# Latent attention and retention as steps between the first projection's weight tiles, and high parts of the tokens written straight from the PSUM banks

## The reference

```python
h = rms_norm(x, attn_norm_w)
r_q, r_k, r_v, r_g, c_q, c_kv, k_pe = split(h @ w_in)   # widths 4 x 512, 256, 128, 32
# retention, 8 heads of 64: decayed scores times values, norm of each head, gate
q, k = rope(r_q), rope(r_k) / 8
o = ((q @ k.T) * decay_mask) @ r_v                      # written here for both chunks at once
y_ret = silu(r_g) * group_norm(o) * ret_gn_w
# latent attention, 8 heads of 64 + 32
q = rms_norm(c_q) @ w_uq;  kv = rms_norm(c_kv) @ w_ukv
s = (q_nope @ k_nope.T + rope(q_pe) @ rope(k_pe).T) * 96 ** -0.5   # causal
y_mla = softmax(s) @ v
x = x + concat(y_ret, y_mla) @ w_out
x = x + conv_ffn(rms_norm(x, ffn_norm_w), ...)
```

## Time and profile before

| | before |
|---|---|
| median of 3 runs | 2361.56 us (2360.82 to 2362.85) |
| the profiled execution | 2360.28 us, its span 2358.6 us |
| mean granted TensorE clock | 0.978 |
| PE busy in the span | 97% |
| DVE busy | 80% |
| ACT busy | 50% |

### The profile page before, as it was taken

The page is one execution under the profiler, slowest core; times in us unless marked ns, Lnnn a source line. Parts: engine busy times, 40 slices in busy tenths (PEclk is TensorE's granted clock), DMA queues, the critical chain, the costliest instruction groups (busy, mean ns, idle before and its releaser), DMA issues.

```text
span 2358.6 us, 34719 instructions
## 1 busy us (share of the span) xinstructions
PE 2283.0 (97%) x13406; PEld 1906.2 (81%) x13406; DVE 1882.3 (80%) x3423; ACT 1187.1 (50%) x1741; POOL 169.3 (7%) x75
## 2 busy tenths in 40 slices
PE   7899999999899999999999999999999999999997
PEld 6789987776788888887777777788888888777786
DVE  8658987577769998888888888769998888888656
ACT  5445554347455555554444444445555554444543
POOL 0000000000014420000000000004440000000000
PEclk9779999999999999999999999999999999999999
DMA  8316676323455655555558896456655555556663
GB/s 316 123 54 230 199 258 233 99 81 108 147 184 188 185 182 173 171 175 169 171 171 285 331 346 216 144 194 188 187 181 176 172 170 170 171 170 238 209 214 123
DMA packets 123186, 442.30 MB, mean 188 GB/s; under 512 B 13696, under 2 KB 16768, under 8 KB 122256
## 3 DMA queue, kind: packets, MB, share of 16 engines
q1 hardware_dynamic: 117288, 425.04, 54.9%
q10 hardware_dynamic: 5736, 15.06, 1.9%
HBM read 436.88 MB, written 3.16 MB: 187 GB/s over the span
## 4 chain that ended last, share of the span: by engine, by line
PE 82%; DVE 12%; ACT 3%; issue 2%; DMA 0%; ACTq 0%; SPq 0%; DVEq 0%
PE psum L410 20%; PE psum L418 14%; PE psum L419 14%; PE psum L420 14%; PE psum L411 10%; DVE spl L2322 3%; PE psum L413 3%; PE psum L2588 3%; DVE acc L1581 1%; PE psum L412 1%; DVE cv L1852 1%; ACT spl L979 1%; ACT cv L1229 1%; PE psum L2529 1%; DVE sm L1997 1%
## 5 line engine op out<-in xcount | busy, mean ns | idle before, releaser
L2322 DVE TENSOR_TENSOR spl<-ring,spl 128x1024 fp32r<-128x1024 f32 (+1 forms) x639 | 784.4, 1229 | 348.1 <-ACT spl L979 346.2
L979 ACT ACTIVATE spl<-ring 128x1024 fp32r<-128x1024 f32 x703 | 739.2, 1053 | 493.3 <-PE psum L413 354.2
L410 PE MATMUL psum<-hT,spl 128*128 128x512 f32 x2016 | 729.8, 400 | 2.4 <-DVE hT L1561 2.4
L411 PE MATMUL psum<-hT,spl 128*128 128x256 f32 x2016 | 566.3, 281 | 0.0
L410 PEld LDWEIGHTS psum<-hT,spl 128*128 128x128 f32 x2016 | 380.8, 189 | 81.3 <-issue 3.0
L418 PE MATMUL psum<-spl,Ws 128*128 128x512 f32 x1024 | 411.5, 402 | 1.8 <-DVE Ws L2360 1.6
L419 PE MATMUL psum<-spl,Ws 128*128 128x512 f32 x1024 | 404.5, 395 | 0.0
L420 PE MATMUL psum<-spl,Ws 128*128 128x512 f32 x1024 | 404.0, 395 | 0.0
L411 PEld LDWEIGHTS psum<-hT,spl 128*128 128x128 f32 x2016 | 382.7, 190 | 9.4
L1508 ACT ACTIVATE Ws<-S 128x256 fp32r<-128x256 f32 x256 | 106.8, 419 | 385.3 <-PE psum L420 380.3
L2648 POOL TENSOR_TENSOR spl<-ring,spl 128x1024 fp32r<-128x1024 f32 x64 | 162.9, 2545 | 1196.6 <-ACT spl L979 1196.6
(11 more groups left out here) (385 smaller groups left out, 3026.0 us busy)
## 6 DMA issues: line engine op xcount, KB each, us to landing
ring<-in_peer_u SPq DMA_DIRECT2D x256, 512.0 KB, 4.0
ring<-in_peer_v SPq DMA_DIRECT2D x256, 512.0 KB, 4.0
vring<-in_ada_w SPq DMA_DIRECT2D x56, 512.0 KB, 6.4
ring<-in_w_up SPq DMA_DIRECT2D x44, 512.0 KB, 4.4
aring<-in_ada_w SPq DMA_DIRECT2D x40, 512.0 KB, 6.0
ring<-in_ab_in SPq DMA_DIRECT2D x32, 512.0 KB, 3.5
ring<-in_peer_wq SPq DMA_DIRECT2D x32, 512.0 KB, 4.6
ring<-in_w_down SPq DMA_DIRECT2D x22, 512.0 KB, 6.0
```

What stands on the lines that cost most here:

```text
L410: q.matmul(b[:, :].rearrange("p (z t) -> p z t", z=2), l[0], r, start=start, stop=False)
L411: return q.matmul(b[:, 0:256], l[1], r[:, 0], start=False, stop=False)
L979: q.activation(P.spl[:, m % SPLITS, 0, 0:w], P.ring[:, m % SLOTS, 0:w], ACT.Copy).then_inc(*P.hi.mark(m))
L2322: q.tensor_tensor(P.spl[:, n % SPLITS, 1, 0:w], P.ring[:, n % SLOTS, 0:w], P.spl[:, n % SPLITS, 0, 0:w].bitcast(F32), ALU.subtract).then_i ...
```

## The change

**Order of tiles.** The latents' chunk comes first, then retention's queries; then `w_uq` and `w_ukv` (tiles 8 to 10), then keys, values and gates (tiles 11 to 22). The output projection begins with the rows of latent attention (`WO_TILE`).

**Steps between tiles.** `pe_in` and the loops of ACT and DVE call, behind a tile (i, p) (chunk i in the new order, tile p), what `MLA_STEPS` and `RET_STEPS` list. A step s of latent attention is the scores of head s, the transposes of head s-2 and the values of head s-4; one of retention is the scores of head s and the values of head s-2. The banks 4 to 7 belong to them, the banks 0 to 3 to the projection, with the transposes of the exponentials and of retention's rotated blocks in banks 0 and 1.

**High parts from the banks.** Where blocks of tokens were scaled to a scratch tile and split there, ACT now writes the scaled high part from the bank (or, at the start, from `xTf`) straight to its place, and DVE makes the low part with one instruction, `split_lo`, out of the same bank.

**Moved beside it.** The copies of the turned keys (`mkT`) and the values (`mv`) go from DVE to ACT. The gates are evicted with Silu in place of a copy and a Silu later. The transfers of tokens come in quarters, `rmask` in halves. Two of the eight modulation steps go from the stage `in` to `wo`. Group norm reads retention's output from banks 2 and 3, and one square root replaces two.

The diff, cut to its core:

```diff
-T_IN, T_UQ, T_UKV, T_WO, T_UP, T_DN, T_AB, T_ABO = 0, 20, 22, 23, 31, 75, 97, 129
+T_IN, T_UQ, T_UKV, T_WO, T_UP, T_DN, T_AB, T_ABO = 0, 8, 10, 23, 31, 75, 97, 129
+IN_CHUNK = (4, 0, 1, 2, 3)
+MLA_STEPS = {(3, 0): (0, 1), (3, 1): (2, 3), (3, 2): (4, 5), (3, 3): (6, 7), (4, 0): (8, 9), (4, 1): (10, 11)}
+RET_STEPS = {(4, 1): (0, 1), (4, 2): (2, 3, 4), (4, 3): (5, 6, 7, 8, 9)}
+WO_TILE = ((0, 2), (0, 3), (1, 2), (1, 3), (0, 0), (0, 1), (1, 0), (1, 1))
+def in_tile(i, p):
+    return T_IN + 4 * i + p + (3 if i >= 2 else 0)
...
-    places = [("in", n) for n in (5, 7, 10, 12, 14, 16, 18, 19)]
+    places = [("in", n) for n in (5, 7, 13, 14, 19, 20)] + [("wo", 4), ("wo", 5)]
...
 def pe_in(q, P):
...
+            if (i, p) == (1, 0):
+                pe_latents(q, P)
+            elif (i, p) == (1, 3):
+                pe_up_latents(q, P)
+            elif (i, p) == (2, 2):
+                pe_mla_queries(q, P)
+            elif (i, p) == (2, 3):
+                pe_mla_keys(q, P)
+            elif i == 3:
+                pe_ret_turn(q, P, p)
+            elif (i, p) == (4, 3):
+                pe_mla_out(q, P)
+            for s in MLA_STEPS.get((i, p), ()):
+                pe_mla_step(q, P, s)
+            for s in RET_STEPS.get((i, p), ()):
+                pe_ret_step(q, P, s)
...
+def pe_mla_step(q, P, s):
...
+    n, nt, nv = heads(s, 0, 2, 4)
+    if n is not None:
+        b = P.ps[4 + n % 2]
+        q.wait_ge(*act.at(("mkT", max(n // 2, n % 2))))
+        if n >= 2:
+            q.wait_ge(*dve.at(("esb", n - 2)))
+        q.matmul(b[:, 0:128], P.mqT[0:96, n, 0:128], P.mkT[0:96, n, 0:128], start=True, stop=True)
+        q.matmul(b[:, 128:384], P.mqT[0:96, n, 128:256], P.mkT[0:96, n, :], start=True, stop=True).then_inc(
+            *pe.mark(("s", n)))
+    if nt is not None:
+        b = P.ps[0 if nt < 6 else 4 + nt % 2]
+        q.wait_ge(*act.at(("x", nt)))
...
+    if nv is not None:
...
+def act_mla_step(q, P, s):
+    pe, act, dve = P.stage("mla")
+    n, nt = heads(s, 0, 2)
+    if nt is not None:
+        q.wait_ge(*pe.at(("turn", nt)))
...
+    if n is not None:
...
+        q.wait_ge(*dve.at(("mx", n)))
...
+def split_lo(q, L, dst, x, scale, *event):
+
+    if scale is None:
+        q.tensor_tensor(dst[1], x, dst[0].bitcast(F32), ALU.subtract).then_inc(*L.mark(*event))
+    else:
+        q.scalar_tensor_tensor(out=dst[1], in0=x, scalar=scale, in1=dst[0].bitcast(F32), op0=ALU.mult,
+                               op1=ALU.subtract).then_inc(*L.mark(*event))
...
     for k in range(8):
-        if k % 4 == 0:
-            q.wait_ge(*P.line(f"xT{k // 4}_loaded").at("xT"))
-        q.tensor_scalar(P.xTf[:, k, :], P.xTf[:, k, :], P.wcol("attn", k), None, ALU.mult).then_inc(*dve.mark())
-        q.wait_ge(*dve.now())
-        hilo(q, dve, P.hT, k, P.xTf[:, k, :], ("hT", k))
-        if k % 2:
+        q.wait_ge(*act.at(("hT", k)))
+        split_lo(q, dve, (P.hT[:, 0, k, :], P.hT[:, 1, k, :]), P.xTf[:, k, :], P.wcol("attn", k), ("hT", k))
+        if k in (1, 3):
             dve_lo(q, P, k // 2)
+    dve_angles(q, P)
+    for i in range(5):
+        for p in range(4):
+            n = in_tile(i, p)
+            dve_lo(q, P, n + 2)
+            if i == 3 and p < 2:
+                dve_ret_rope(q, P, 1, p)
+            for s in MLA_STEPS.get((i, p), ()):
+                dve_mla_max(q, P, s)
+            if (i, p) == (4, 2):
+                dve_mla_out(q, P)
+            dve_ada(q, P, ("in", n))
+            for s in RET_STEPS.get((i, p), ()):
+                dve_ret_mask(q, P, s)
+            if n == 3:
+                dve_rstd(q, dve, act, P.ss1, P.rs1, 1024, ("sq1", 1), "1")
+            elif (i, p) == (1, 0):
+                dve_latents(q, P)
+            elif (i, p) == (1, 2):
+                q.wait_ge(*act.at("cos"))
+                for tb in range(2):
+                    dve_key_rope(q, P, tb)
+            elif (i, p) == (1, 3):
+                for tb in range(2):
+                    dve_lo(q, P, T_UKV + tb)
+                    dve_ret_rope(q, P, 0, tb)
+                dve_lo(q, P, T_UKV + 2)
...
```

More of the change, by code:

```diff
@@ L523, in pe_latents, with pe_up_latents @@
-    s0 = pe_take(q, P, T_UKV)
-    q.wait_ge(*dve.at(("cT", 2)))
+def pe_up_latents(q, P):
+    pe, act, dve = P.stage("lat")
+    for k in range(2):
+        sl = pe_take(q, P, T_UQ + k)
+        q.wait_ge(*dve.at(("cT", 2 * k)))
+        for i, (lo, hi) in enumerate(((0, 480), (480, 768))):
+            for tb in range(2):
+                t = mm3(q, P.ps[4 + 2 * i + tb][:, 0:hi - lo],
+                        cut(both(P.cT), lambda v: v[:, k, tb * 128:(tb + 1) * 128]), cut(sl, lambda v: v[:, lo:hi]),
+                        k == 0, k == 1)
+                if k or (i and tb):
+                    t.then_inc(*pe.mark(("mq", i, tb), *([("used", T_UQ + k)] if i and tb else [])))
+    sl = pe_take(q, P, T_UKV)
@@ new lines, in pe_ret_step @@
+def pe_ret_step(q, P, s):
+    iact = P.stage("in")[1]
+    pe, act, dve = P.stage("ret")
+    n, nv = heads(s, 0, 2)
+    if n is not None:
+        b = P.ps[4 + n % 2]
+        r = 64 * (n % 2)
+        qh, kh = P.qkT[r:r + 64, n // 2, :], P.qkT[r:r + 64, 4 + n // 2, :]
+        if n < 2:
+            q.wait_ge(*P.stage("mla")[1].at(("pT", 6 + n)))
+            q.wait_ge(*iact.at(("qkT", 3)))
+        else:
+            q.wait_ge(*dve.at(("mask", n - 2)))
+        q.matmul(b[:, 0:256], kh[:, 0:128], qh, start=True, stop=True)
+        q.matmul(b[:, 256:384], kh[:, 128:256], qh[:, 128:256], start=True, stop=True).then_inc(*pe.mark(("s", n)))
+    if nv is not None:
+        b = P.ps[2 + nv // 4]
+        o = [b[:, tb * 256 + nv % 4 * 64:tb * 256 + nv % 4 * 64 + 64] for tb in range(2)]
+        v = [P.P5[:, tb, 1024 + nv * 64:1088 + nv * 64] for tb in range(2)]
+        m = P.rT[:, nv % 2, :]
+        if nv == 0:
+            q.wait_ge(*iact.at(("ev", 3, 1)))
+        q.wait_ge(*dve.at(("mask", nv)))
+        q.matmul(o[0], m[:, 0:128], v[0], start=True, stop=True)
+        q.matmul(o[1], m[:, 128:256], v[0], start=True, stop=False)
+        q.matmul(o[1], m[:, 256:384], v[1], start=False, stop=True).then_inc(*pe.mark(("o", nv)))
@@ L629, in pe_turns, with pe_mla_out @@
+def pe_mla_out(q, P):
+    mdve = P.stage("mla")[2]
+    pe = P.stage("wo")[0]
+    for g in (2, 3):
+        for k in (2 * g, 2 * g + 1):
+            for tb in range(2):
+                if k == 4:
+                    q.wait_ge(*mdve.at(("mix", tb)))
+                o = k % 2 * 256 + tb * 128
+                t = q.transpose(P.ps[4 + g][:, o:o + 128], P.mixed[:, tb, k * 128:(k + 1) * 128], P.ident[:, :])
+        t.then_inc(*pe.mark(("turn", g)))
 def pe_turns(q, P, pe, done, banks, nk, src, *first):
@@ L1085, in act_latents, with act_up_latents @@
+    for ss, name in ((P.ss2, "2"), (P.ss3, "3")):
         q.wait_ge(*dve.at("ms" + name))
         q.activation(ss, ss, ACT.Sqrt).then_inc(*act.mark("sd" + name))
+def act_up_latents(q, P):
+    pe, act, dve = P.stage("lat")
+    act_hi(q, P, T_UKV + 1)
     q.wait_ge(*dve.at("rs2"))
@@ L1823, in dve_wo @@
+    q.wait_ge(*P.line("x_loaded").at("x"))
+    sums(0, 0)
+    sums(0, 1)
     for tb in range(2):
```

728 lines of the change are left out of this document (346 added, 382 removed).

## The result

| | before | changed |
|---|---|---|
| median | 2361.21 us (2360.82 to 2362.85, 4 runs) | 2336.97 us (2335.28 to 2338.21, 4 runs) |
| ratio, 95% interval | | 0.9896 (0.9878 to 0.9913) |
| profiled execution | 2360.28 us, span 2358.6 | 2336.15 us, span 2334.8 |
| mean granted clock | 0.978 | 0.987 |

The change wins 24.2 us. The forecast was 2344.5, its range 2335 to 2357; what happened is nearest to its rival (a), a clock that stays full, priced at 2337.5.

The account below looks back on a forecast made before the run. The front part was taken as bound by a chain of small dependent steps, mostly at half clock. Stretch and start -26.0, tail +1.5, low parts -1.2, semaphore gaps +1.5, clock +7: -17 us, 2344.5 us, range 2335 to 2357.

Parts of the forecast that it names:

- rival (a): Attention and retention between tiles: the clock stays full; -24 us, 2337.5 us; chance 0.25.
- The walk: First projection through output projection, slot by slot: 118.6 work, 1.2 half-clock start, 15.2 waits; 135.0 us instead of 160.2.
- low parts of tiles 8 to 12: Projection behind the latents: VectorE alone sets the pace; TensorE waits 0.6, 0.8, 1.4, 0.5 and 0.6 us.
- The attention slots: Tiles 15 to 20: a loop of ScalarE and VectorE makes TensorE wait, 3.5 us in all.
- the output slots: Output projection: low parts held back by retention's norms (1.0, 1.4) and turned retention heads (1.3), 3.7 us of waits.
- The clock: First score to last retention head, 60 us: a quarter at half clock costs 7 us; bounds 0 and 38.
- (c): VectorE's strict queue order costs more: waits of 25 us instead of 15, same clock; 2354 us; chance 0.20.
- (d): Small matmuls hold the clock down through the whole stretch: 38 us lost against 24 won; 2375.5 us; chance 0.07.
- (e): Waits move without shortening, every slot costing 2 us more than in (c); about 2360 us; chance 0.06.
- the signs that the prediction named: Profile: last output matmul at 145 to 152 us, clock 0.8 to 0.95 from 60 to 122, low-part waits about 7.
- The bank low parts: Up projection: one-instruction low parts out of banks, every 0.46 us, win 1.2 us (bounds 0.5 and 2).
- The tail: Behind the output projection: VectorE's two last modulation steps ahead of the first residual sum add 1.5 us (bounds 0 and 4.8).

Follow-up runs that it names:

- experiment 11: Changed kernel with the first four modulation loads (2 MB) issued behind tile 7 instead of tile 5: 2333.87 us.
- experiment 5: Changed kernel with all ten retention steps in a row behind the projection's last tile: 2341.88 us.
- experiment 1: Changed kernel with all attention steps, then all retention steps, behind the projection's last tile, none between tiles: 2344.05 us.
- experiment 2: Kernel of experiment 1 with attention's chain one head apart (transposes of head s-1, values of s-2) instead of two: 2356.74 us.
- experiment 10: Kernel of experiment 9 with ScalarE's next two high parts after the second block's squares, and VectorE reading the fold before its low part: 2333.86 us.
- experiment 7: Kernel before the change, with only the high parts from banks and one-instruction low parts in output and up projection: 2362.29 us.
- experiment 8: Changed kernel with the up projection's eight blocks scaled to scratch, cast and subtracted as before the change: 2336.63 us.
- experiment 9: Changed kernel with the last two modulation steps behind output tiles 2 and 4 instead of 4 and 5: 2334.19 us.
- experiments 3: Changed kernel with attention's chain one head apart instead of two, steps still between tiles (ten instead of twelve): 2340.76 us.
- experiment 4: Changed kernel with attention steps in fours behind every second tile instead of in twos behind six: 2337.39 us.
- experiment 6: Kernel of experiment 5 with three unread 512-column matmuls added to each retention step, 30 in all: 2340.19 us.

## Why the prediction was right, and where it was not

**The walk.** It put the end of the stretch at 8.4 + 135.0 = 143.4 us; the last output matmul ended at 143.1. The first matmul was forecast at 8.4 and came at 8.49. Single waits were other than told: TensorE waited 2.94 us at 23.8 for the latents' eviction, because `x` landed at 20.97 behind 2 MB of modulation weights (experiment 11), a place that the walk did not have; 1.13 us before tile 1; and not at all before tile 7, where it had 2.5. For the low parts of tiles 8 to 12 it waited about 2 us (0.4, 1.14, 0.21, 0.21) instead of 3.9. The attention slots held 3.3 us (1.12, 0.66 and 0.83 at the transposes, 0.73 ahead of the projection's last chunk) against 3.5; the output slots 2.9 (0.71, 1.09, 1.10) against 3.7. Together 12.3 us of waits against the 15.2 forecast, with 3.4 us at half clock near 27 that the walk did not have. The sum agrees better than its terms, and that its end is met within 0.3 us is in part luck.

**The clock: the term that was wrong.** "But small matmuls pull the clock down even when nothing idles, and here 4 to 7 us of them lie between tiles of 2.73 us ... I expect it to fall in some slots": +7 us, measured 0 from 30 to 140 us in the profiled execution. The row behind it, 87.4 to 101 at 0.50, is retention's, and begins only behind the fall at 87.2; the wait of 0.78 us ahead of that fall was not read. Experiment 5 shows that the row applies when retention's heads stand in a row (+4.9 us), and experiment 1 that it does not apply to attention, which keeps 1.00 for 17.4 us. Attention's low clock before came from its chain's waits (experiment 2). The longest run of retention left in the changed kernel, with eight transposes ahead of it, lasts 7.4 us, at 1.00. Of (c), (d) and (e) nothing was seen.

Rival (a) is not certain in every execution. In the trace of experiment 10, whose attention slots are the changed kernel's, the clock fell at 79.0 at the end of a wait of 0.84 us, as the forecast has it; that execution took 2336.21 us where its median was 2333.86. So a small part of the 7 us is real in some executions.

Of the signs that the prediction named, the last output matmul came before the stretch that it gave (143.1, not 145 to 152), the clock from 60 to 122 us above it (1.00, not 0.8 to 0.95), and the waits for low parts from 24 to 47 us were 1.75 us, not 7.

The Trainium skill ("TensorE: Matmul & The Clock Gate", HAM oscillation) lays the loss of the clock to idle gaps. That falls go with waits (2.94 us at 23.8 in the changed kernel, 2.05 and 0.79 in experiment 2) agrees in kind, but all of these are shorter than the about 3 us that the prediction takes from that page; and retention in the kernel before, at half clock for 13.6 us with TensorE busy all the time, does not agree.

**What carries the gain.** The prediction did not split it, and took the tiles between the steps for its ground. The runs split 19.8 us of it: one head apart and behind the projection 2356.7; two heads apart -12.7 (2344.1); retention and attention between the tiles -7.1 (2337.0), of which retention alone is 4.9. In the other order the shares change: between the tiles first -16.0 (2340.8), then two heads apart -3.8. Both steps keep the waits short, and each takes most of what the other could, so neither has a share of its own. The first 4.5 us, from 2361.2 to 2356.7, are the rest of the change, the latents and turned blocks between tiles, less what the tail gives back; no run takes these apart.

**The bank low parts.** The term was -1.2 us (0.5 to 2); its pace was forecast at 0.46 and measured at 0.40, better. At its place it was worth what the term says: 1.1 us at the second up tile in experiment 7, 1.5 in experiment 8. In the whole it was worth nothing, since TensorE loses as much again on the way to the second fold. The step that was wrong is that a gain at the head of the up projection lasts to its end.

**The tail.** The term was +1.5; from the fold to the first up matmul it took 9.99 us instead of 7.59, +2.4. Half of it is VectorE's last modulation step, ending at 140.16 ahead of the first sum (experiment 9, 8.75). From fold to fold it is +2.2 (145.0 instead of 142.8), against the +0.3 that tail and low parts had together.

## What to carry to other kernels

Price the clock by the row of the same kind of work, and read what stood ahead of a fall as well as what follows it: retention's low stretch did not carry over to attention, and attention's own came from its waits. Before weaving a chain of small steps into other work, put its stages one step further apart: that alone took 12.7 us here, against 16.0 for the weaving alone, and with it only 7.1 us were left for the weaving. Don't add up such shares from single edits. A part that shortens an engine's work is worth what its place on the path is worth: ask who frees the banks, and whether the time that it wins is waited for again further on.

## What the runs showed of the hardware

The same eight attention heads run at either clock, and stay there: at 1.00 through 17.4 us with TensorE busy for 15.41, and at 0.50 for 21.3 us with TensorE busy for 20.27, after a fall that came with two waits of 2.05 and 0.79 us. At half clock the engine is busier and still is not granted the full clock. Windows of experiment 2, up to the fall and after it:

```profile
84.70:89.00 4.30, 2.25 (x15) 1.79 (x14) 3.27 (x7) 3.63 (x8) 0.00 (x0) 1.00 0.80 263
89.70:111.00 21.30, 20.27 (x85) 18.65 (x86) 7.04 (x19) 10.44 (x34) 0.00 (x0) 0.50 0.03 10
```

A wait does not decide it alone. At one place, the turning of the latents, all of these kernels run the same instructions; behind a wait of 2.5 to 2.6 us the clock fell in experiments 3 and 4 and stayed at 1.00 in experiments 1, 5 and 10. The row of experiment 4, then of experiment 5:

```profile
26.05 1.34 PE L532 MATMUL psum<-ident,P 128*128 128x128 f32 x6 [2.51 <-ACT P L1168]
```

```profile
26.15 1.05 PE L532 MATMUL psum<-ident,P 128*128 128x128 f32 x6 [2.56 <-ACT P L1168]
```

In the same way a wait of 0.83 us at 79 us had no fall in the changed kernel and one of 0.84 had one in experiment 10. So one trace with a full clock does not show that a place is safe.

And work can be added for nothing: thirty full matmuls in experiment 6 paid for themselves with the clock.
